# Three DVE and ACT steps moved in a hybrid attention block: the gate of the last quarter, two table loads and one softmax normalisation

## What is computed

```python
h = rms_norm(x, norm_in_w)
proj = jnp.einsum('bsd,dc->bsc', h, w_in)
a_q, a_k, a_v, a_g, b_cq, b_ckv, b_kr, b_g = split_columns(proj)
...
out_a = swa_sink_attention(qa, ka, va, sinks_a) * jax.nn.silu(a_g)
qb = jnp.einsum('bsr,rc->bsc', rms_norm(b_cq, q_a_norm_w), w_q_b)
...
out_b = mla_attention(qb_nope, qb_rope, kb_nope, kb_rope, vb) * jax.nn.silu(b_g)
mixed = jnp.concatenate([out_a, out_b], axis=-1)
x = x + jnp.einsum('bsc,cd->bsd', mixed, w_out)
return rms_norm(x, final_norm_w)
```

## Time and profile before

| | us |
|---|---|
| median of 3 runs | 717.15 |
| lowest, highest | 716.98, 717.79 |
| the profiled execution | 716.98 |
| its span, first to last instruction | 715.0 |

### The profile page before, as it was taken

How to read it: one execution, slowest core, us unless ns; L and a number is a source line. 1 busy time by engine, 2 the same in 40 slices (tenths; PEclk the granted TensorE clock), 3 DMA queues, 4 the chain that set the end, 5 groups by cost and what they waited for, 6 DMA issues and landing times.

```text
span 715.0 us, 9017 instructions
## 1 busy us (share of the span) xinstructions
PE 683.7 (96%) x3282; PEld 567.6 (79%) x3282; DVE 316.6 (44%) x515; ACT 303.2 (42%) x573; POOL 321.6 (45%) x150
## 2 busy tenths in 40 slices
PE   5999999999979999999999997999999999999995
PEld 4888887888858888888888786878778888888884
DVE  6957120980693553543443576776852110100013
ACT  6722232212124564564464475566653141322233
POOL 3654443444433233433443335545675275464630
PEclk9999999999999999999999999999999999999999
DMA  8632222333221122212322312210121932232215
GB/s 286 218 125 98 103 88 89 89 97 110 88 88 61 60 89 89 88 60 89 96 81 89 119 59 89 89 61 29 60 60 60 352 119 89 88 117 88 89 48 217
DMA packets 21588, 73.47 MB, mean 103 GB/s; under 512 B 2352, under 2 KB 2480, under 8 KB 21424
## 3 DMA queue, kind: packets, MB, share of 16 engines
q1 hardware_dynamic: 18144, 66.07, 27.2%
q10 hardware_dynamic: 3408, 6.90, 2.7%
HBM read 68.77 MB, written 4.19 MB: 102 GB/s over the span
## 4 chain that ended last, share of the span: by engine, by line
issue 40%; PE 32%; POOL 18%; DVE 5%; ACT 3%; DMA 1%; POOLq 0%; SPq 0%; DVEq 0%; ACTq 0%
POOL w_lo L244 18%; PE bank L946 10%; PE bank L950 10%; PE bank L949 10%; DVE t L811 1%; DVE pb L852 1%; PE bank L1142 1%; DVE st_b L844 1%; DMA xs<-x_t 1%; DVE ptb_lo L857 1%; ACT pb L475 1%; PE bank L1132 0%; PE bank L1133 0%; DMA w_raw<-w_stream 0%; ACT x_hi L323 0%
## 5 line engine op out<-in xcount | busy, mean ns | idle before, releaser
L244 POOL TENSOR_TENSOR w_lo<-w_raw,w_hi 128x1024 fp32r<-128x1024 f32 x109 | 266.4, 2448 | 324.3 <-ACT w_hi L317 323.7
L946 PE MATMUL bank<-x_hi,w_hi 128*128 128x512 f32 x520 | 204.9, 394 | 2.9 <-DVE t L631 2.9
L317 ACT ACTIVATE w_hi<-w_raw 128x1024 fp32r<-128x1024 f32 x110 | 116.1, 1058 | 210.0 <-PE bank L946 190.7
L950 PE MATMUL bank<-x_lo,w_hi 128*128 128x512 f32 x520 | 202.9, 390 | 0.0
L949 PE MATMUL bank<-x_hi,w_lo 128*128 128x512 f32 x520 | 202.5, 389 | 0.0
L946 PEld LDWEIGHTS bank<-x_hi,w_hi 128*128 128x128 f32 x520 | 97.8, 188 | 23.3 <-DVE t L631 3.3
L950 PEld LDWEIGHTS bank<-x_lo,w_hi 128*128 128x128 f32 x520 | 97.6, 188 | 20.7
L949 PEld LDWEIGHTS bank<-x_hi,w_lo 128*128 128x128 f32 x520 | 97.7, 188 | 19.5 <-issue 0.5
L946 PE MATMUL bank<-w_hi,mx_hi 128*128 128x512 f32 x256 | 101.0, 394 | 0.0
L949 PE MATMUL bank<-w_hi,mx_lo 128*128 128x512 f32 x256 | 100.0, 391 | 0.0
L950 PE MATMUL bank<-w_lo,mx_hi 128*128 128x512 f32 x256 | 99.9, 390 | 0.0
(11 more groups left out here) (177 smaller groups left out, 911.1 us busy)
## 6 DMA issues: line engine op xcount, KB each, us to landing
w_raw<-w_stream SPq DMA_DIRECT2D x110, 512.0 KB, 3.3
xs<-x_t SPq DMA_DIRECT2D x8, 512.0 KB, 4.4
y<-x_nat ACTq DMA_DIRECT2D x4, 1024.0 KB, 9.1
out<-y SPq DMA_DIRECT2D x8, 512.0 KB, 3.6
fw<-final_w ACTq DMA_DIRECT2D x1, 1024.0 KB, 15.6
cos_b<-tables ACTq DMA_DIRECT2D x2, 256.0 KB, 2.7
sin_b<-tables ACTq DMA_DIRECT2D x2, 256.0 KB, 2.9
cos_r<-tables ACTq DMA_DIRECT2D x1, 256.0 KB, 3.5
```

The source lines that it names most:

```text
L244: pool.tensor_tensor(w_lo[:, s % HL, :], w_raw[:, s % RAW, :], w_hi[:, s % HL, :].bitcast(F32), ALU.subtract)\
L317: act.activation(w_hi[:, s % HL, :], w_raw[:, s % RAW, :], ACT.Copy).then_inc(w_hi_ready, 1)
L946: ins = pe.matmul(dst, ah, bh, start=start, stop=False)
L950: return pe.matmul(dst, ah, bl, start=False, stop=stop)
```

## The change

Three steps move; no instruction is added or removed.

- DVE: `gate(3)` moves from behind the second F of pair 0 to the split of pair 0, between the low part of the second query tile and those of the keys.
- ACT: the wait for `gated` 8 and the two table DMAs move from the fourth F of pair 0 to the point ahead of pair 0's first step.
- DVE: `before_split` leaves the condition for `a_normalise`. For t = 1 and 2 the unit's scores stand two half steps ahead of 13, so nothing moves. For t = 0 the normalisation of unit 3 goes behind `a_split_q(1)`.

```diff
@@ scalar
             high_part(PB0 + AHEAD + 2, PB0 + AHEAD + 2)
+            act.wait_ge(gated, 8)
+            act.dma_start(cos_b[1][:, :], tables[:, P:P + SEQ]).then_inc(rot_landed, 16)
+            act.dma_start(sin_b[1][:, :], tables[:, P + SEQ:P + 2 * SEQ]).then_inc(rot_landed, 16)
             for p in range(PAIRS):
...
                     elif step[0] == "F":
-                        if p == 0 and f == 3:
-
-                            act.wait_ge(gated, 8)
-                            act.dma_start(cos_b[1][:, :], tables[:, P:P + SEQ]).then_inc(rot_landed, 16)
-                            act.dma_start(sin_b[1][:, :], tables[:, P + SEQ:P + 2 * SEQ]).then_inc(rot_landed, 16)
@@ vector
-                    before_split = hf == Q_SPLIT_AT and t < 3
-                    if last is not None and (before_split or hf in AT_TRANSPOSE[t] or hf - 2 in AT_SCORES[t] or hf in AT_SCORES[t]):
+                    if last is not None and (hf in AT_TRANSPOSE[t] or hf - 2 in AT_SCORES[t] or hf in AT_SCORES[t]):
                         a_normalise(t, last)
                         last = None
...
             b_tile_low(6)
+            gate(3)
             for j in (0, 3, 1, 2):
                 b_tile_low(j)
...
-                    if p == 0 and step == "F" and f == 2:
-                        gate(3)
```

## The result

The changed kernel takes **723.01 us** (median, 722.26 to 723.71), the kernel before 717.40 beside it (716.98 to 717.79). The ratio is 1.008, with a 95% interval of 1.0066 to 1.0093: slower by 5.6 us. That is outside the predicted range of 717.7 to 722.0, on the side that was forecast. Two executions of the kernel before, run beside the last three experiments, took 1148.64 and 3923.61 us and are left out of its median there.

A forecast was written before the change was run, and what follows sets the result against it. PE, busy 96% of the span, was taken as the bound. Normalisation +4.25, gate -1.5 and table DMAs 0 sum to 2.75 us more, forecasting 719.9 us, range 717.7 to 722.0.

The forecast's parts named there:

- Normalisation behind the split: Quarter 0: DVE normalises only after the query split, held beside POOL, so PE's transposes start 4.25 us late.
- Gate, where it leaves, and T1: Mixer B: T1's 3.69 us gap is consumed, T1 0.5 us earlier plus 1.0 for the clock; gate's move -1.5 us.
- Gate, where it arrives: Split of pair 0: POOL holds the gate pair about 5.5 us; S0 gap 3.1 us, first F +3.16 us.
- Table DMAs: ACT ahead of pair 0's first step: moving the two table loads costs 0, with 0.5 us as upper bound.
- The clock in the new gaps: PE's gaps in quarter 0 (4.2 us) and ahead of S0 (3.1 us): forecast sum charges no clock fall there.
- The likeliest case: Whole kernel: the delays and gains as summed, no clock fall in the new gaps, 719.9 us; chance 42%.
- rival 2: Clock falls in mixer B behind S0's gap, too or instead: 1.3 us more, 721.2 alone, 722.5 with quarter 0's; chance 10%.
- The price of a fall: PE's work behind a new gap: each fall to the lower clock costs 1.3 us, the price of T1.

The follow-up runs named there:

- the last three experiments: The changed kernel measured again, then with unread matmuls filling quarter 0's gap, then also the gap ahead of S0: 722.98, 721.32 and 719.44 us.
- the change again: The whole change, unaltered, measured once more against the kernel before on the same chip as the filled kernels: 722.98 us, ratio 1.008.
- both filled: Changed kernel plus 16 unread matmuls in quarter 0's gap and 12 ahead of S0: 719.44 us, 1.0028 to the kernel before.
- the condition alone: Kernel before with only the normalisation of unit 3 in quarter 0 moved behind the query split: 723.11 us, ratio 1.007.
- the gate with its filler: Kernel before with gate and table DMAs moved and 12 unread matmuls ahead of S0, normalisation unmoved: 715.55 us, ratio 0.9967.

## Why the prediction missed, step by step

- **Normalisation behind the split, +4.25.** Right. The transposes started 38.11 us behind the first score, 4.28 more than before, the split was held as in the earlier trace rows, and nothing behind it absorbed the delay: with quarter 0's gap filled the two stages are 4.4 to 4.6 us over before. That the clock time of 253.05 matches the 253.03 worked out is in part luck; the profile of the change again, with the same delay, has 251.86.
- **Gate, where it leaves, and T1.** Right. T1 has no wait; with the clock kept, mixer B is 1.5 us shorter, the size that was forecast. Its two parts came out as 0.9 us for the earlier T1 and 0.6 behind it (both filled), where 0.5 and 1.0 were worked out. Where the new gap at S0 was not filled, its low clock took this back.
- **Gate, where it arrives.** Right. The pair took 5.44 us for 5.5 from the earlier trace rows, S0's gap was 2.85 for 3.1, the first F's wait 0.91 for 1.1 at the upper clock. Each multiplication ended 0.55 us behind one of POOL's two subtractions (429.40 behind 428.85, 432.16 behind 431.62), as in the rows.
- **Table DMAs, 0.** Not contradicted: 717.45 and 717.36, with intervals of 0.6 us to either side.
- **The clock in the new gaps: the step that failed.** The likeliest case, at 42%, had it stay up in both. It fell in both. This was the half of rival 2 in which both fall, for which I had written 722.5, half of 10%, and which was left out of the range. The reasoning had two faults. It set a gap of 2.9 us in which the clock had not fallen against 3.69 in which it had, and took the end of the span (4.7 us without a fall) as evidence for the side wanted. At the end of the span the clock did fall, just behind the row that was read; PE's last instruction ends at 707.3:

```profile
712.00:714.00 2.00, 0.00 (x0) 0.00 (x0) 0.00 (x0) 0.00 (x0) 0.00 (x0) 0.59 1.02 410
```

It falls there in all 13 profiles, 2.1 to 5.1 us behind PE's last instruction, and this one is the latest of them. And one execution without a fall says little: in the changed kernel the same unchanged gap of 2.9 us ahead of quarter 0 is followed by the row below.

```profile
208.00:210.00 2.00, 2.00 (x6) 1.58 (x5) 2.00 (x2) 0.98 (x1) 1.94 (x2) 0.50 0.00 0
```

- **The price of a fall: mis-sized.** 1.3 us was taken from T1, where the low clock ended after about 3.4 us and so met only 3 us of work. Here it lasted 6.8 us in quarter 0 in one profiled execution of the changed kernel and 3.4 in the other, and the stage was 163.00 - 160.82 = 2.2 and 162.24 - 160.82 = 1.4 us over the filled one. By the medians a fall costs 1.7 and 1.9 us, so two cost 3.5 and not 2.6: 719.4 + 3.5 = 722.98. With 1.3 each, the case would have been 0.5 us short.

Two things stay **open**. Executions of one kernel differ by 1.1 to 3 us, often in groups, and a profile shows one of them. Part of this is how long the clock stays low: the condition alone took 722.0 us twice, at a mean granted clock of 0.991, and 723.1 to 723.2 three times, at 0.989; the two traces of the changed kernel and the long T1 stretch above point the same way. But the mean clock does not order the times by itself: the gate with its filler took 714.5 to 715.4 us at 0.994 and 715.7 to 715.9 at 0.997. Some of the spread lies at the start: the first score of quarter 0 came at 213.7 to 215.2 in the traces, and at 214.95, late among them, in the one of the kernel before. What sets it is not known. For the same reason the stages of one trace and the difference of the medians do not agree to better than about 1.6 us (the changed kernel: +7.2 by stages, +5.6 by medians; both filled: +3.1 and +1.9). The other open thing is why the filler in quarter 0 hardly lowered the median with the condition alone, but did in the whole change; so the 1.7 us for quarter 0 rests on one pair of kernels.

## What to carry to other kernels

A new gap on a TensorE that is otherwise full should be priced at its length and the clock behind it, unless several executions show that a gap of this length is harmless; in these kernels a fall cost 1.3 to 2.2 us by stages and 1.7 to 1.9 by medians, up to about half of PE's time at the lower level. Before a step is moved, look in the timelines for what the other engines do at its new place: the same 1.4 us of DVE work cost 5.4 us beside POOL and, in two pieces and a few instructions earlier, delayed nothing. To tell a delay from its clock, fill the gap with matmuls that nobody reads.

## What the runs showed of the hardware

- TensorE's granted clock fell in PE's gap of 4.1 us in quarter 0 or 1.0 us behind it (three unfilled profiles out of three), and in the gap of 2.85 to 2.87 us ahead of S0 or up to 2.4 us behind it (five unfilled profiles out of five); at T1, with a gap of 3.6 to 3.8 us, in four out of four. With the 2.9 us ahead of quarter 0 it fell in 10 of 13 profiles, and not in that of the kernel before. With a gap of 2.84 us in quarter 0, 2.62 ahead of the first F and 1.6 at T1 it did not fall (one profile each, two for the last).
- A fall may be free: the one ahead of quarter 0 is followed by a wait for the split queries, which is 2.2 us in the three profiles without the fall and 0.5 to 0.6 in the ten with it: the wait takes the lost time up.
- Low stretches lasted 3.4 us (kernel before at T1, gate moved alone, the changed kernel's second profile in quarter 0) or 6.8 us (its first profile, at both places; its second at S0; the condition alone in quarter 0; at T1 with the normalisation between the two subtractions). The same gap had either length in different executions.
- Two DVE multiplications with both operands in SBUF against two POOL subtractions took 5.44 us instead of 1.28, while POOL's pair took 5.17 instead of 4.74: DVE bears nearly all of it when it comes second.
- Sixteen 512-wide matmuls on unused data take 3.8 us and are enough to keep the clock at 1.00 over a gap of 4.1 us; twelve take 2.93 and do the same for one of 2.9.
